# Weights in a new order on the ring: no loads beside the inverse and the chunk walk, values by token block, early output gate panels

## The chip, the cores and the metric

The kernel runs on one core of a Trainium2 chip. Its engines are TensorE (PE: matmuls, with its weight loads shown as PEld), VectorE (DVE), ScalarE (ACT), GpSimd (POOL) and SyncE (SP), which here issues the weight loads. The metric is device time in microseconds, the median of the runs.

## The reference

Two blocks work on x of 256 tokens by 1024 in float32. The first is RWKV-7 time mixing, a recurrence over the tokens, and then block-sparse attention; the second an mLSTM with an MLP and a latent attention (MLA) with an MLP, each modulated by rows that come from one vector c:

```python
x = x + rwkv7_time_mix(rms_norm(x, norm_a[i]), mu_a[i], w_in_a[i], ...)
...
x = x + moba_attention(rms_norm(x, norm_b[j]), w_in_b[j], q_norm_b[j], w_out_b[j], kb, vb, kmean, cos, sin)
...
cond = jax.nn.silu(c)
for l in range(DEPTH):
    ada = cond @ ada_w[l] + ada_b[l]
    sh1, sc1, g1, sh2, sc2, g2 = jnp.split(ada, 6, axis=-1)
    h = modulate(rmsnorm(x, norm_g[l, 0]), sh1, sc1)
    ...
    x = x + g1[:, None, :] * rmsnorm(y, norm_g[l, 1])
    h = modulate(rmsnorm(x, norm_g[l, 2]), sh2, sc2)
    y = sqrelu_mlp(h, mlp_w1[l], mlp_w2[l])
    x = x + g2[:, None, :] * rmsnorm(y, norm_g[l, 3])
```

## The kernel before

**Weights.** All weights come from memory in panels of 2 MB, in one fixed order (`order`), into a ring of four slots. SP issues panel i once panel i-4 is released (L1286 to L1292). A weight panel is worked on in two units. ScalarE writes the high part of a unit to a page (`split`, L1356, page_parts), VectorE writes the low part back into the ring slot (L2019, slot_parts), and TensorE does three matmuls for each product (`three`, L455 to L457: high by high, high by low, low by high). So a weight slot is released only by the last matmul that reads it. The 256 tokens are two token blocks of 128 (`tb`). Some products take each unit for both token blocks at once (`split_tok`, `split_T`), others go through a whole matrix for token block 0 and then again for block 1 (`split_blocks`), and a slot is then held until block 1 has used it; a function called between the units puts transposes there.

**Conditioning.** cond @ ada_w takes 28 panels of 512 columns. Most are summed on VectorE, a quarter of a panel at a time (`ada`, L1993, "ada_rows" in the order). Some go to TensorE (`ada_direct`, L595), 16 matmul records for a panel, and ScalarE copies the row (L1449), which TensorE turns to columns (`ada_turned`, L608). The row has one place in memory.

**The stages.** First block: projections; small 64x64 matmuls (L758) that build an inverse for each chunk; then the chunk walk, where the state goes from chunk to chunk (L813 to L900); wo_a; the attention; wo_b. SP holds conditioning panel 5 until the inverse's last step ("X", 5, 3), so the panels behind it load beside the chunk walk. Second block: norm and transposes of x (hT_c), q2, k2, gates, v2, then eight heads of mLSTM with the output gate's units (og) between them; then two direct conditioning panels, the transposes of the heads' output (h2T), and `mlp`: wo_c by token block, the new x and its norm, the transposes of block 0 (L537) ahead of wo_c's last unit for block 1, and the products up and w2 by turns. MLA and its MLP follow in the same way.

**What is fixed.** Each engine runs its instructions in the order they are written, and waits stand in them. ScalarE's and VectorE's splits are written out by hand among their other work: in `mlp` the splits of up's first panel stand ahead of the sum of squares of the branch's output (L1396). The gate rows of the second block go through eight diagonal matrices (`gate_diagonal`, L2469), which `spread` multiplies by ones.

## Time and profile before

| | before |
|---|---|
| median of 3 runs | 1048.17 us (1045.05 to 1049.97) |
| profiled execution: time, span | 1047.87 us, 1046.1 us |
| granted TensorE clock, mean | 0.99 |
| instructions | 19356 |
| DMA | 205.40 MB, 95 panels of 2048 KB |

The span is the time from the first to the last instruction in the trace, and t = 0 is its start. Times in the rows are microseconds. The busy share is an average over all stages: what stops TensorE has to be read stage by stage. A wait is put down to the engine that came last; "issue" stands for time in which the engine waited for nothing that the profile shows.

### The profile page before, as it was taken

Reading aid. Unit: us, or ns where it says so; the run is one execution under the profiler, and the core shown is the slowest. Engines: PE = TensorE matmul, PEld = TensorE weight load, DVE = VectorE, ACT = ScalarE, POOL = GpSimd, SP = SyncE. Lnnn points to the kernel's source line nnn. Section 1 sums busy time; section 2 is a strip of 40 time slices with the busy share of each in tenths; the row PEclk is TensorE's granted clock in tenths of the full one; section 3 lists DMA queues with packets and bytes.
Section 4 is the critical chain, followed back from the end, with each engine's and each line's share of the span. In section 5 each row is a group of like instructions: output and inputs, shape, how many; then the busy total and the mean of one; then the engine's idle time right before and its main releaser. Section 6 shows DMA issues by size and latency. Waiting matters only on the chain.

```text
span 1046.1 us, 19356 instructions
## 1 busy us (share of the span) xinstructions
PE 993.2 (95%) x8274; PEld 864.8 (83%) x8274; DVE 752.1 (72%) x1277; ACT 525.6 (50%) x798; POOL 36.4 (3%) x33
## 2 busy tenths in 40 slices
PE   5999999968999999999999999999999899999996
PEld 4788899967788888788867899999688788999995
DVE  6789889577889958646589665676587895664544
ACT  3358431316454677455366445454466855445442
POOL 0000044200000100000000000000000000000000
PEclk9999999999999999999999999999999999999999
DMA  9674410492456550564264477776646444476411
GB/s 379 248 284 161 162 43 4 162 389 100 154 211 219 221 242 11 232 242 161 81 242 161 170 294 303 287 291 264 240 164 215 188 161 161 172 296 256 171 72 41
DMA packets 15222, 205.40 MB, mean 196 GB/s; under 512 B 1816, under 2 KB 1816, under 8 KB 2976
## 3 DMA queue, kind: packets, MB, share of 16 engines
q1 hardware_dynamic: 14544, 202.55, 50.5%
q10 hardware_dynamic: 592, 1.61, 0.5%
q8 instruction: 66, 1.08, 0.4%
q14 instruction: 20, 0.16, 0.0%
HBM read 203.10 MB, written 1.05 MB: 195 GB/s over the span
## 4 chain that ended last, share of the span: by engine, by line
PE 83%; DVE 10%; ACT 3%; issue 2%; DMA 1%; SPq 0%; DVEq 0%; ACTq 0%
PE bank L455 20%; PE bank L457 20%; PE bank L456 20%; PE bank L758 5%; PE bank L404 4%; DVE slot_parts L2019 2%; PE bank L661 1%; PE bank L562 1%; DMA ring<-in_stream 1%; PE bank L739 1%; PE bank L634 1%; DMA pc<-in_params 1%; PE bank L623 1%; PE bank L900 1%; PE bank L537 1%
## 5 line engine op out<-in xcount | busy, mean ns | idle before, releaser
L455 PE MATMUL bank<-page_parts 128*128 128x512 f32 (+3 forms) x1222 | 428.8, 351 | 6.8 <-DVE page_parts L2301 2.2
L2019 DVE TENSOR_TENSOR slot_parts<-ring,page_parts 128x2048 fp32r<-128x2048 f32 (+2 forms) x117 | 261.4, 2251 | 53.4 <-ACT page_parts L1356 52.9
L457 PE MATMUL bank<-page_parts 128*128 128x512 f32 (+2 forms) x750 | 291.4, 389 | 0.0
L456 PE MATMUL bank<-slot_parts,page_parts 128*128 128x512 f32 (+2 forms) x750 | 290.9, 388 | 0.0
L455 PEld LDWEIGHTS bank<-page_parts 128*128 128x128 f32 x1222 | 232.3, 190 | 36.5 <-issue 3.7
L1356 ACT ACTIVATE page_parts<-ring 128x2048 fp32r<-128x2048 f32 (+2 forms) x121 | 225.0, 1884 | 52.6 <-PE bank L457 28.1
L457 PEld LDWEIGHTS bank<-page_parts 128*128 128x128 f32 x750 | 141.3, 188 | 29.0
L456 PEld LDWEIGHTS bank<-slot_parts,page_parts 128*128 128x128 f32 x750 | 141.8, 189 | 26.8
L1434 ACT ACTIVATE arena<-bank 128x512 f32<-128x512 f32 (+2 forms) x134 | 74.2, 575 | 127.2 <-PE bank L457 67.0
L457 PE MATMUL bank<-page_parts,slot_parts 128*128 128x256 f32 x472 | 133.6, 283 | 0.0
L456 PE MATMUL bank<-page_parts 128*128 128x256 f32 x472 | 133.6, 283 | 0.0
L1993 DVE CUSTOM_DVE_ANT_0 ring<-ring,small 128x1024 f32<-128x1024 f32 x88 | 104.1, 1229 | 0.0
L456 PEld LDWEIGHTS bank<-page_parts 128*128 128x128 f32 x472 | 90.6, 192 | 0.5
L457 PEld LDWEIGHTS bank<-page_parts,slot_parts 128*128 128x128 f32 x472 | 90.6, 192 | 0.0
L2573 DVE TENSOR_TENSOR page_parts<-arena,page_parts 128x512 fp32r<-128x512 f32 x24 | 16.6, 692 | 80.4 <-ACT page_parts L1773 80.4
L1769 ACT ACTIVATE arena<-bank 128x512 f32<-128x512 f32 x24 | 14.3, 597 | 117.4 <-PE bank L457 117.4
L758 PE MATMUL bank<-arena 64*64 64x64 f32 x1792 | 53.2, 219 | 2.0 <-issue 2.0
L758 PEld LDWEIGHTS bank<-arena 64*64 64x64 f32 x1792 | 52.8, 136 | 2.1 <-issue 2.1
L404 PE MATMUL bank<-arena,ring 128*128 128x256 f32 x192 | 41.9, 380 | 0.0
L404 PEld LDWEIGHTS bank<-arena,ring 128*128 128x128 f32 x192 | 36.4, 190 | 5.4 <-DMA ring<-in_stream 0.4
L562 PE MATMUL bank<-cc,arena 128*128 128x128 f32 x142 | 19.3, 292 | 18.2 <-DVE arena L1961 13.4
L2249 DVE TENSOR_TENSOR arena<-arena,bank 128x512 f32<-128x512 f32 x36 | 24.0, 683 | 16.9 <-PE bank L758 16.7
(318 smaller groups left out, 1114.2 us busy)
## 6 DMA issues: line engine op xcount, KB each, us to landing
ring<-in_stream SPq DMA_DIRECT2D x95, 2048.0 KB, 8.0
arena<-in_x SPq DMA_DIRECT2D x2, 512.0 KB, 4.3
arena<-in_gn ACTq DMA_DIRECT2D x2, 512.0 KB, 4.4
...
```

What stands on the lines that cost most here:

```text
L404: ins = mm(b[:, half * T:(half + 1) * T], weights[:, k, ct * P:(ct + 1) * P], src[:, k, :], start=(k == 0), stop=(k == k_tiles - 1))
L455: mm(out, a[0], b[0], start=start, stop=False)
L456: mm(out, a[0], b[1], start=False, stop=False)
L457: return mm(out, a[1], b[0], start=False, stop=stop)
L562: ins = nc.tensor.transpose(b[:, jj * T + tb * P:jj * T + (tb + 1) * P], src[:, tb, j * P:(j + 1) * P], ident)
L758: ins = mm(b[q * LC:(q + 1) * LC, j * LC:(j + 1) * LC], lhs(q, j), rhs(q, j), start=True, stop=True)
L1356: act(unit_parts(n)[0], unit_values(n)[1], ACT.Copy).then_inc(ac.step("w_hi"), 1)
L1434: act(dst, bank(product)[:, 0:n].rearrange("p (a b) -> p a b", a=dst.shape[1]) if len(dst.shape) == 3 else bank(product)[:, 0:n], kw.get(" ...
L1993: V.tensor_tensor_reduce(W, W, cond_row, 1.0, 0.0, ALU.mult, ALU.add, accum_out=ADA[:, at:at + 1]).then_inc(dv.step("ada_done" if ct == 3 ...
L2019: tt(unit_parts(n)[1], lo, hi, ALU.subtract).then_inc(dv.step("w_lo"), 1)
L2249: tt(dst[:, g], dst[:, g], bank((name, l, g))[:, :].rearrange("p (j t) -> p j t", j=8), ALU.subtract).then_inc(dv.frees((name, l, g)), 1)
L2573: tt(AF_LO[:, n % 2, 2 * i:2 * i + 2, :], a, hi, ALU.subtract).then_inc(dv.step("relu2"), 1)
```

## The change

1. **Ring and conditioning, first block.** Two panels, not six, are summed between g and wo_a. VectorE's 16 quarters in the inverse and the walk are gone. SP holds wo_a's second panel until chunk 2's state ("S", 2). The direct panel before yT is gone. In wo_a VectorE makes the low parts of yT ahead of a weight split, and ScalarE the high parts.
2. **Attention.** Three summed panels, not two, stand behind q1; VectorE sums 12 quarters there, not 8. ScalarE splits wo_b's first unit two heads later.
3. **wo_b and the mLSTM's entry.** wo_b goes by token block. hT_c is turned block by block, beside wo_b and v2. v2 comes first, by token block, then gates, q2, k2; og's panels are asked for before the heads.
4. **Gates.** One multiplication gives a column of eight gates; TensorE spreads it by a broadcast operand against the identity, with as many matmuls.
5. **Heads.** VectorE sums conditioning quarters in seven of the eight heads.
6. **MLP 0.** The ring's order at its entry is wo_c's first panel, direct, direct, wo_c's second; before it was direct, direct, and wo_c's two. Two more panels are summed in its loop.
7. **MLA.** Three direct panels, not two, two of them with four groups of 32 columns; three places for the row. One split is moved behind the norm of cq.

In all there are five direct and 23 summed panels, where there were six and 22. The diff, cut to its core:

```diff
@@ -500,12 +501,19 @@
                             ins.then_inc(filled((*name, 0)), 1)
                     ins.then_inc(unit_used((*name, 1) if i else None), 1)
-            def split_blocks(name, src, pages, ready, between=None, banks_of=None):
+            def block_panels(name, pages, after_first=None):
                 first, panels_of = len(units), []
                 for half in range(2):
                     split_panel((name, half), pages, by_k=True)
                     panels_of.append(order[-1])
+                    if half == 0 and after_first:
+                        after_first()
+                return first, panels_of
+            def split_blocks(name, src, pages, ready, between=None, banks_of=None, loaded=None):
+                first, panels_of = loaded or block_panels(name, pages)
                 for tb in range(TB):
                     bs = [claim((name, half, tb), None if banks_of is None else banks_of[2 * tb + half]) for half in range(2)]
...
-                i = ada_panel("ada")
-                ada_direct_of.append(i)
+                return slot, ada_panel("ada"), order[-1]
+            def ada_direct(reserved=None, pause=None, groups=2):
+                slot, i, entry = reserved or direct_panel()
+                ada_direct_of.append((i, groups))
                 b = claim(("ada_row", i))
                 pe.wait_ge(sem(f"slot_loaded{slot % SLOTS}"), 16 * (slot // SLOTS + 1))
                 W = ring[:, slot % SLOTS, :].rearrange("p (k n) -> p k n", k=KT)
+                width = P // groups
                 for k in range(KT):
...
+                    ins = mm(b[at:at + width, :], cond[:, k:k + 1].to_broadcast([P, width]), W[:, k, :], start=(k < groups),
+                             stop=(k >= KT - groups), tile_position=(0, at))
                 ins.then_inc(filled(("ada_row", i)), 1)
-                panel_used()
+                entry[1] = pn.last
             ada_turns = [0]
             def ada_turned():
...
@@ -748,7 +764,7 @@
             grams(1)
             turn("at", lambda j: AR[:, j, 0, :])
             project_rows("g", G_PAGES, 1)
-            ada(6)
...
-            ada_direct()
             turn_block("yT", Yr, 0, lambda g: (sem("y_gated"), g + 1))
             stage[0] = "attention"
             def beside_wo_a(tb, n):
-                if (tb, n) == (0, 1):
-                    ada_turned()
-                elif (tb, n) == (1, 0):
+                if (tb, n) == (1, 0):
                     turn_block("yT", Yr, 1, lambda g: (sem("y_gated"), 2 + g + 1))
                 elif (tb, n) == (1, 2):
...
                     ada(1)
-            ada(2)
...
@@ -974,24 +987,35 @@
             attention("at1", NH, HD, scores1, V1)
             transposes("o1T", O1, ready=lambda i: (sem("o1"), 1 + i // 3))
             stage[0] = "wo_b"
-            for half in range(2):
-                split_tok(("wo_b", half), split_parts(O1_PAGES), first_of(15, 16, 3), wait=("o1T_split", 0) if half == 0 else None)
+            def beside_wo_b(tb, n):
+                if (tb, n) == (1, 2):
+                    turn_block("hT_c", XN, 0, lambda g: (sem("xn"), 5))
+            def beside_v2(tb, n):
+                if (tb, n) == (0, 2):
+                    turn_block("hT_c", XN, 1, lambda g: (sem("xn"), 6))
+            def from_first(*pages):
...
                     for jj in range(4):
-                        pe.wait_ge(sem("diag"), 8 * i + 4 * half + jj + 1)
-                        ins = mm(b[:, jj * P:(jj + 1) * P], ones, DIAG[:, 4 * half + jj, :], start=True, stop=True)
+                        j = 4 * half + jj
+                        ins = mm(b[:, jj * P:(jj + 1) * P], gcol[:, j:j + 1].to_broadcast([P, P]), ident, start=True, stop=True)
                     ins.then_inc(filled(("gb", i, half)), 1)
...
             stage[0] = "mlstm"
-            for name in ("q2", "k2"):
-                split_T((name,), split_parts(MLSTM_PAGES), first_of(6, 14, 11), wait=("hT_c_split", 0) if name == "q2" else None)
-                if name == "q2":
-                    ada(1)
+            split_blocks("v2", split_parts(MLSTM_PAGES), from_first(6, 14, 1, 2), lambda tb, k: (sem("hT_c_split"), 2 * tb + k // 4 + 1),
+                         beside_v2)
             b = claim("gates")
...
+                ins.then_inc(filled("gate_cols"), 1)
+            ada(1)
+            split_T(("q2",), split_parts(MLSTM_PAGES), from_first(11, 16))
+            split_T(("k2",), split_parts(MLSTM_PAGES), from_first(13, 15), between=gate_columns)
+            og_pages = from_first(8, 11, 16, 13)
...
+                split_panel(("og", half), og_pages, by_k=True)
+            ada(2)
+            pe.wait_ge(*evacuated(("k2", 1)))
...
@@ -1173,17 +1192,20 @@
                     mm(b[:, 129:258], w[:, P:T], V2[:, 0, g, :], start=True, stop=False)
                     mm(b[:, 129:258], w[:, T:T + P], V2[:, 1, g, :], start=False, stop=True).then_inc(filled(("num", g)), 1)
             rotation["banks"] = kept
-            ada_direct()
-            ada_direct()
+            stage[0], reserved = "mlp0", []
+            loaded = block_panels("wo_c", from_first(15, 16, 3, 12), lambda: reserved.extend([direct_panel(), direct_panel()]))
+            for panel_of in reserved:
+                ada_direct(panel_of)
...
-            mlp(0, "wo_c", split_parts(H2_PAGES), "h2T_split", lambda tb, n: ada_turned() if (tb, n) == (0, 2) else None)
+            mlp(0, "wo_c", split_parts(H2_PAGES), "h2T_split", lambda tb, n: ada_turned() if (tb, n) == (0, 2) else None, loaded)
             ada_direct()
+            ada_direct(groups=4)
             stage[0] = "mla"
             q_a = split_spans("q_a", (0, 1536, 4, 15), (1536, 3072, 4, 16))
-            ada_direct((sem("x_sq"), 9))
...
@@ -1287,8 +1310,8 @@
                 if i >= SLOTS:
                     sp.wait_ge(*order[i - SLOTS][1])
-                if name == ("ada_rows", 5):
-                    sp.wait_ge(*finished(("X", 5, 3)))
+                if name == ("wo_a", 1):
+                    sp.wait_ge(*finished(("S", 2)))
                 sp.dma_start(ring[:, i % SLOTS, :], stream[i]).then_inc(sem(f"slot_loaded{i % SLOTS}"), 16)
...
             y_squares_of(1, 0)
             y_squares_of(1, 1)
-            split(unit_of["wo_a", 0] + 2)
-            ada_direct()
             halves_of("yT", 0, Y_PAGES)
             group_root(1)
             split(unit_of["wo_a", 0] + 3)
-            ada_turned()
             page_used.update({14: finished(("y", 1, 1)), 1: finished(("y", 1, 1)), 2: evacuated(("y", 1, 1)), 6: (sem("y_reduced"), 4)})
...
             page_used.update({p: finished(("v1", 1, 1)) for p in (15, 16)})
             u = unit_of["wo_b", 0]
-            attention("at1", NH, HD, 0.125, {n + 1: [(u + n // 4, n % 4)] for n in range(8)})
+            attention("at1", NH, HD, 0.125, {n + 3: [(u + n // 4, n % 4)] for n in range(8)})
...
                 if c == 2:
                     split(unit_of["wo_a", 0])
                 p = ("S", c)
@@ -2314,11 +2337,11 @@
             reduced(0)
             gated(0)
             group_norm(0)
-            split(unit_of["wo_a", 0] + 1)
             reduced(1)
             lows_of("yT", 0, Y_PAGES)
+            split(unit_of["wo_a", 0] + 1)
+            gated(1)
             split(unit_of["wo_a", 0] + 2)
-            gated(1)
             group_norm(1)
             lows_of("yT", 1, Y_PAGES)
...
             next_unit(("k1", 0, 0))
-            ada(8)
+            ada(12)
             def attention(name, heads, dvd, scale, O, early, between=None, gathered=None):
...
                     split(unit_of["cq"] + 1)
-            norm()
-            ada(2)
-            split_h("hT_c", MLSTM_PAGES)
-            for n in range(4):
-                next_unit(("q2", 0))
-                if n == 0:
-                    ada(2)
-                elif n == 1:
-                    modulation(4, 6, ())
-                    gate_diagonal(0)
+            modulation(4, 6, ())
+            gate_column(0)
+            u = unit_of["v2", 0]
+            for tb in range(TB):
+                add_to_x("wo_b", (tb,))
+                split(u + 2 * tb)
+                norm_block(tb)
+                split(u + 2 * tb + 1)
+                split_rows("hT_c", MLSTM_PAGES, 0, tb)
+            split(unit_of["q2",] + 1)
+            ada(4)
             dve.wait_ge(sem("gate_ln"), 1)
...
                         finish_head(g - 1)
+                if h < 7:
+                    ada(1 if h else 2)
                 if h == 7:
                     split(unit_of["wo_c", 0])
```

**VectorE, inverse's end to the chunk walk.** L2260 is the walk's preparation of a gate row, L1993 conditioning quarters (each with a short second instruction, left out here), L2312 the state's new value for a chunk. Before:

```order
L2260 TENSOR_TENSOR arena<-arena 128x1024 [waits dve_steps]
L1993 ISA ring,ADA<-ring,small 128x1024 [waits slot_loaded2]
L1993 ISA ring,ADA<-ring,small 128x1024
L1993 ISA ring,ADA<-ring,small 128x1024 [waits slot_loaded3]
L2312 TENSOR_TENSOR arena<-bank,small 128x512 [waits bank_full6]
L2260 TENSOR_TENSOR arena<-arena 128x1024
L1993 ISA ring,ADA<-ring,small 128x1024 [waits slot_loaded0]
L2312 TENSOR_TENSOR arena<-bank,small 128x512 [waits bank_full7]
L2019 TENSOR_TENSOR slot_parts<-ring,page_parts 128x2048 [waits w_hi]
L2312 TENSOR_TENSOR arena<-bank,small 128x512 [waits bank_full6]
```

Now, where L2284, L2335, L2045 and L2300 are the same lines as L2260, L2312, L2019 and L2276:

```order
L2284 TENSOR_TENSOR arena<-arena 128x1024 [waits dve_steps]
L2335 TENSOR_TENSOR arena<-bank,small 128x512 [waits bank_full6]
L2284 TENSOR_TENSOR arena<-arena 128x1024
L2335 TENSOR_TENSOR arena<-bank,small 128x512 [waits bank_full7]
L2045 TENSOR_TENSOR slot_parts<-ring,page_parts 128x2048 [waits w_hi]
L2335 TENSOR_TENSOR arena<-bank,small 128x512 [waits bank_full6]
L2300 TENSOR_REDUCE small<-arena 128x8 [waits y_square] x2
```

The quarters and their waits for slots are gone; the weight split stays between the second and third chunk.

**TensorE, from wo_b to the first product of the mLSTM.** L457 is the last of wo_b, L595 the direct panel, L562 the transposes of both blocks, L608 its row turned, L465 to L467 q2. Before, without repeats:

```order
L457 MATMUL bank<-page_parts 128x512
L595 MATMUL bank<-ring,small 64x512 [waits slot_loaded1,bank_free0]
L562 MATMUL bank<-cc,arena 128x128 [waits bank_free1,xn]
L562 MATMUL bank<-cc,arena 128x128 [waits bank_free2]
L562 MATMUL bank<-cc,arena 128x128 [waits bank_free3]
L608 MATMUL bank<-cc 128x1 [waits bank_free0,bank_free5]
L465 MATMUL bank<-page_parts 128x256 [waits hT_c_split,w_lo,bank_free6]
L466 MATMUL bank<-page_parts 128x256
L467 MATMUL bank<-page_parts,slot_parts 128x256
```

Now, the transposes (L545) of block 0 stand in wo_b's second block, v2's first unit (L454 to L456) follows wo_b at once, and block 1's transposes stand after v2's second unit:

```order
L545 MATMUL bank<-cc,arena 128x128 [waits xn,bank_free6]
L545 MATMUL bank<-cc,arena 128x128 [waits xn,bank_free7]
L454 MATMUL bank<-page_parts 128x512
L454 MATMUL bank<-page_parts 128x512
L454 MATMUL bank<-page_parts 128x512 [waits w_lo,hT_c_split,bank_free1,bank_free0]
L454 MATMUL bank<-page_parts 128x512 [waits hT_c_split,w_lo]
L545 MATMUL bank<-cc,arena 128x128 [waits xn,bank_free2]
L545 MATMUL bank<-cc,arena 128x128 [waits xn,bank_free3]
L454 MATMUL bank<-page_parts 128x512 [waits w_lo]
```

The direct panel and its row are gone, and so is the place where TensorE has nothing but transposes to do.

**ScalarE, the entry of MLP 0.** L1356 splits wo_c, and from the x2 row on up's first panel; L1449 copies a conditioning row, L1462 scales h2T, L1396 is the sum of squares of wo_c's output. Before, without repeats:

```order
L1356 ACTIVATE page_parts<-ring 128x2048 [waits pe_steps,slot_loaded3]
L1356 ACTIVATE page_parts<-ring 128x2048 [waits bank_full1,slot_loaded0]
L1449 ACTIVATE cc<-bank 128x512 [waits bank_full2]
L1462 ACTIVATE arena<-bank,pc 128x256 [waits bank_full4]
L1442 ACTIVATE ADA<-bank 128x4 [waits bank_full0]
L1449 ACTIVATE cc<-bank 128x512 [waits bank_full3]
L1356 ACTIVATE page_parts<-ring 128x2048 [waits bank_full1,slot_loaded0]
L1442 ACTIVATE ADA<-bank 128x4 [waits bank_full4]
L1356 ACTIVATE page_parts<-ring 128x2048 [waits bank_full1,slot_loaded1] x2
L1396 ACTIVATE arena,small<-bank 128x512 [waits bank_full0]
L1396 ACTIVATE arena,small<-bank 128x512 [waits bank_full1]
```

Now (L1379, L1474, L1487, L1465 and L1419 are the same lines):

```order
L1379 ACTIVATE page_parts<-ring 128x2048 [waits pe_steps,slot_loaded2]
L1379 ACTIVATE page_parts<-ring 128x2048 [waits bank_full3,slot_loaded1]
L1474 ACTIVATE cc<-bank 128x512 [waits bank_full6]
L1487 ACTIVATE arena<-bank,pc 128x256 [waits bank_full0]
L1465 ACTIVATE ADA<-bank 128x4 [waits bank_full4]
L1474 ACTIVATE arena<-bank 128x512 [waits bank_full7]
L1379 ACTIVATE page_parts<-ring 128x2048 [waits bank_full3,slot_loaded1]
L1465 ACTIVATE ADA<-bank 128x4 [waits bank_full4]
L1379 ACTIVATE page_parts<-ring 128x2048 [waits bank_full3,slot_loaded2] x2
L1419 ACTIVATE arena,small<-bank 128x512 [waits bank_full0]
L1419 ACTIVATE arena,small<-bank 128x512 [waits bank_full1]
```

The rows and their order are the same; the slots that the splits wait for are others. The panels in the ring, each with the panel whose slot it takes:

```
before: direct <- v2_0, direct <- v2_1, wo_c0 <- og0, wo_c1 <- og1, up00 <- direct, up01 <- direct, w2_0 <- wo_c0, summed <- wo_c1, up02 <- up00
after:  wo_c0 <- og0, direct <- og1, direct <- summed, wo_c1 <- summed, up00 <- wo_c0, up01 <- direct, summed <- direct, w2_0 <- wo_c1, summed <- up00, up02 <- up01
```

## Rows read from the trace of the kernel before

**Rows 1.** The page: busy time of each engine.
```profile
PE 993.2 (95%) x8274; PEld 864.8 (83%) x8274; DVE 752.1 (72%) x1277; ACT 525.6 (50%) x798; POOL 36.4 (3%) x33
```
**Rows 2.** Windows: stretch, us, busy PE, PEld, DVE, ACT, POOL, PEclk, DMA share, GB/s.
```profile
145.30:197.50 52.20, 52.20 (x1792) 52.20 (x1793) 43.40 (x59) 14.87 (x26) 22.31 (x16) 1.00 0.07 21
203.60:249.30 45.70, 33.49 (x986) 32.42 (x982) 29.19 (x46) 11.64 (x18) 0.00 (x0) 0.89 0.71 286
```
**Rows 3.** TensorE's waits, 197 to 250: total, times, longest; largest and smallest of six.
```profile
PE bank L838 <- issue: 2.9, 1, 2.9
...
PE bank L838 <- DVE arena L2312: 0.8, 1, 0.8
PE bank L827 <- issue: 0.7, 1, 0.7
```
**Rows 4.** Windows in the chunk walk: first and last of three slow stretches, then full clock.
```profile
206.80:210.20 3.40, 3.40 (x71) 3.40 (x69) 2.79 (x4) 0.00 (x0) 0.00 (x0) 0.50 1.03 439
...
237.50:240.90 3.40, 3.27 (x62) 3.27 (x64) 2.01 (x1) 1.35 (x1) 0.00 (x0) 0.51 0.05 14
240.90:249.30 8.40, 8.24 (x292) 8.06 (x289) 5.59 (x13) 4.93 (x7) 0.00 (x0) 1.00 0.01 4
```
**Rows 5.** Panel loads of L1292, 197.5 to 199.9: durations, first and last start, landing.
```profile
L1292 SPq DMA_DIRECT2D ring<-in_stream x4: 328/434/516, 197.8 to 199.2; - x4
...
DMA to landing us min/median/max: 8.6/15.3/22.0
```
**Rows 6.** TensorE's timeline before wo_a: start, us, line, shapes, idle before.
```profile
249.27 3.65 PE L595 MATMUL bank<-ring,small 128*64 128x512 f32 x16
252.85 1.09 PE L537 MATMUL bank<-cc,arena 128*128 128x128 f32 x8
255.09 0.47 PE L455 MATMUL bank<-page_parts 128*128 128x512 f32 x1 [1.15 <-DVE page_parts L2301]
```
**Rows 7.** TensorE's timeline from wo_b to q2.
```profile
426.89 0.39 PE L456 MATMUL bank<-slot_parts,page_parts 128*128 128x512 f32 x1
427.12 0.39 PE L457 MATMUL bank<-page_parts 128*128 128x512 f32 x1
427.43 3.65 PE L595 MATMUL bank<-ring,small 128*64 128x512 f32 x16
...
435.54 0.36 PE L465 MATMUL bank<-page_parts 128*128 128x256 f32 x1 [0.69 <-DVE page_parts L2066]
```
**Rows 8.** VectorE's timeline before the first head.
```profile
479.56 8.90 DVE L2019 TENSOR_TENSOR slot_parts<-ring,page_parts 128x2048 fp32r<-128x2048 f32 x4 [3.62 <-ACT page_parts L1356]
```
**Rows 9.** VectorE's timeline in the MLA: the gate diagonals.
```profile
763.54 1.66 DVE L2469 TENSOR_SCALAR arena<-cc,small 128x128 f32<-128x128 f32 x8
```
**Rows 10.** TensorE's longest wait in the MLA, 740 to 800.
```profile
PE bank L562 <- DVE arena L2696: 1.7, 1, 1.7
```
**Rows 11.** Panel loads of L1292, 520 to 524.5, columns as in rows 5.
```profile
L1292 SPq DMA_DIRECT2D ring<-in_stream x1: 327/327/327, 523.4 to 523.4; - x1
...
DMA to landing us min/median/max: 7.8/7.8/7.8
```
**Rows 12.** SP's timeline, 550 to 560.
```profile
556.56 0.33 SPq L1292 DMA_DIRECT2D ring<-in_stream  x1
```
**Rows 13.** ScalarE's timeline at wo_c.
```profile
531.20 1.91 ACT L1356 ACTIVATE page_parts<-ring 128x2048 fp32r<-128x2048 f32 x1 [1.11 <-DMA ring<-in_stream]
...
534.21 3.02 ACT L1462 ACTIVATE arena<-bank,pc 128x256 f32<-128x256 f32 x8 [0.61 <-PE bank L562]
...
547.13 3.71 ACT L1356 ACTIVATE page_parts<-ring 128x2048 fp32r<-128x2048 f32 x2
```
**Rows 14.** The chain of waits, 520 to 562: start, us, what.
```profile
537.35 0.49 PE bank L455
...
560.42 1.06 PE bank L537 x8
```
**Rows 15.** Windows: the slow stretch in wo_c, columns as in rows 2.
```profile
537.90:541.30 3.40, 3.40 (x9) 2.63 (x8) 3.37 (x4) 1.68 (x1) 0.00 (x0) 0.50 0.86 369
```

193 lines of the change are left out of this document (95 added, 98 removed).

## The prediction

> **What bounds the kernel now.** I read the page's busy shares first: TensorE is busy 95% of the span [rows 1]. So the time is TensorE's work plus the places where it stands still, and a change pays only where it takes one of those away, or costs where it makes one. Then I looked for the places by the busy time of stretches and by TensorE's waits in them. Two are large. One is the chunk walk of the first block (203.6 to 249.3), where TensorE is busy 33.49 of 45.70 us while the inverse before it, with 1792 matmuls in 52.20 us, has no gap at all [rows 2]. The other is the border between wo_b and the mLSTM, 427.5 to 435.5 [rows 7]. Third I read the ring, since the change puts its panels in another order: each panel is issued only when the panel four places ahead of it has been released, and SP issues strictly in that order, so a late release also holds all that stand behind it.
>
> **A. No load in the walk: -13.3.** In the walk the waits name "issue", six of them from 2.9 to 0.7 us, together 11.3 us [rows 3]; the inverse has none. They are not waits for data. What differs is the load: the four panels issued at 197.8 to 199.2 [rows 5] keep the DMA engines 71% busy there, against 7% in the inverse [rows 2]. Beside them TensorE fell three times to a granted clock of 0.50 (1.2 GHz) for 3.4 us; there 71 or 62 matmuls were done where 8.40 us at full clock hold 292, or 28.8 ns each [rows 4]. That is 2.0 and 1.8 us of work in 3.4, so a stretch costs some 1.4 and the three 4.0. Without both: 45.7 - 11.3 - 4.0 = 30.4 us; from the other side 986 matmuls by 28.8 ns and 1.0 us of waits on VectorE and banks make 29.4, so the two agree. Gain 15.3. The new hold lets wo_a's second panel and k1's go once chunk 2's state is done, some 6.6 us before the walk's end. One issue wait of the mean size (11.3/6 = 1.9) comes back: 13.3. Bounds: 0 if the waits do not come from the loads, 15.3 if none comes back.
>
> The Trainium skill ("Runtime: NRT & Kernel Launch", Instruction fetch mechanics) says that instructions are fetched block by block by the engine's own queue, and that this is hidden because the engine dispatches more slowly than the fetch fills. By that rule no issue wait could come from a load, and A would be the clock's 4.0 at most. The trace speaks against it here: six such waits of 11.3 us with loads, none without [rows 2, 3].
>
> VectorE loses 16 quarters of conditioning (the ISA rows at L1993) in inverse and walk. TensorE waits for VectorE only 0.8 us in the walk, so I count nothing.
>
> **B. Direct panel off, VectorE's order in wo_a: -1.4.** Before wo_a TensorE ran 16 matmuls for a conditioning row (3.65 us), turned yT (1.09) and then waited 1.15 for VectorE's low part [rows 6]. Without the 3.65 us TensorE stands ready earlier, but the chain y, norm, low part on VectorE hardly moves; what moves is that the low part of yT now stands ahead of a weight split of 2.3 us (L2019). I take 1.4 of the 3.65+1.15; bounds 0 and 4.8.
>
> **C. wo_b by token block, values first: -3.1.** Between wo_b's last matmul (427.12, the next 0.23 later, as 426.89 to 427.12 shows) and q2's first stand 8.0 us: the direct panel's 3.65, then turns and small matmuls with waits for VectorE, the last of 0.69 [rows 7]. In the new order the two turns stand inside wo_b and v2, 2 x 1.09 [rows 6], so 8.0 - 2.2 = 5.8 goes. Against it: VectorE's four og splits end at 488.5, where the first head's work starts, and the last split was preceded by a wait of 3.62 for ScalarE [rows 8]; so 3.6 is all that VectorE can be brought forward, and with TensorE there 5.8 earlier it comes 2.2 late. ScalarE's halves of wo_b begin two heads later in the attention: 0.5 for the first unit. Together -5.8+2.2+0.5 = -3.1. Bounds -5.8 and +2 (the norm of block 0 has two units of 12 matmuls by 0.23 as cover, 5.5 us; if it needs 8, 2.5 comes back at each of the two turns).
>
> The gate's eight multiplications (1.66 us together) become one; TensorE's matmuls stay as many. In the MLA the eight [rows 9] stand ahead of a wait of TensorE of 1.7 [rows 10], which G counts; at the other places TensorE's waits name nothing near them, so they count nothing.
>
> **D. wo_c's second panel comes third: +9.7.** Before, the ring had direct, direct, wo_c0, wo_c1; now wo_c0, direct, direct, wo_c1. The slot that came free last was og1's, at 523.41. Then only wo_c1 waited for it, and landed 7.8 us later at 531.2 [rows 11]. Now the first direct panel stands in that slot, and behind it on SP the second and wo_c1: all three leave at 523.4 to 524. Queued panels land one by one: of the four at 197.8 to 199.2 the first took 8.6, the last 22.0 [rows 5], so 206.4 and 221.2 and 4.9 us between two. So 531.6, 536.5 and 541.4. ScalarE splits wo_c1's first half before it copies the conditioning row and scales h2 [rows 13] (the order of both kernels stands under the change): 541.4 + 1.91 + 0.6 = 543.9 for the scaling against 534.21, and TensorE's first wo_c matmul stood 3.14 behind that, at 537.35 [rows 14]: 547.0, 9.7 later. The two direct panels, on TensorE from 531.6 and 536.5, are through by then (3.65 each).
>
> **E. The MLP's first panel waits for wo_c0: +17.2 more.** up(0,0) had a direct panel's slot, free before wo_c begins. Now it has wo_c0's, which is released when TensorE has gone through that panel for the second token block; before, this release let another panel go at 556.56 [rows 12]. With D: 556.56 + 9.7 = 566.2, landed 7.8 later, 574.0. On ScalarE the two splits of that panel stand ahead of the squares of the branch's output, and VectorE's low parts stand ahead of its sums, and both are ahead of the new x, its norm and the turn. Before, from the start of that split (547.13, [rows 13]) to the turn (560.42, [rows 14]) it took 13.3 us, all of it work in a row. 574.0 + 13.3 = 587.3, against 560.42: 26.9 in all, 17.2 beyond D. TensorE stands at that turn, with only the last unit of wo_c ahead.
>
> **F. What follows: +3.4.** up(0,2) has up(0,1)'s slot and not up(0,0)'s. Between the two only w2's first panel is left, 48 matmuls by 0.23, 10.9 us, and the load (7.8), issue (0.3), high and low splits (1.9+2.3) make 12.3: +1.4, with what is queued on SP 1.7. And after 18 us of standing TensorE a slow stretch is likely: before, one came at 537.90 after the short gaps there, 3.4 us at 0.50 [rows 15], so 1.7.
>
> **G. MLA: +0.3.** A third direct panel takes the slot of w2's last, whose release comes late in the MLP, and its load of 7.8 [rows 11] is likely to end about 1 us behind the place where TensorE wants it; the gate's shorter work and the split moved behind cq's norm take part of the 1.7 wait [rows 10]. Bounds -1 and +2. The direct panels in four groups of 32 columns have no row: at least 8 matmuls of 0.23 (1.83), as the present form's 16 records in 3.65 show half that rate; I take 1.83 and keep 7.3 (twice the old) as the other end, which is in the range.
>
> The Trainium skill ("TensorEngine Tiling (Array Packing)", When to Use Tiling) names four column groups for a stationary side of 32 columns. By it four of the matmuls run side by side, a quarter of the time. The row with two groups shows 3.65 us for 8 products of 512 columns [rows 7], which is no better than one after another; by the rule the sum would be lower by up to 2.
>
> Sum: -13.3 -1.4 -3.1 +9.7 +17.2 +3.4 +0.3 = +12.8 us. The profiled span of 1046.1 becomes 1058.9; that execution took 1047.87, 1.8 more than its span and 0.3 under the median of 1048.17. So 1060.7, and I say 1061.
>
> **Rivals.**
> 1. *The MLP's first panel is not late* (the other side). If its slot comes free by 549, so that it has landed when ScalarE gets to it (547.13 + 9.7 = 556.9), E's 17.2 falls: 1061 - 17 = 1044, and 2.2 of F with it (no long stand, no slow stretch): 1042, faster by 0.6%. For it: only the release rule holds it, no data. Against it: the low part of wo_c0 is written into its slot and read until the second block's matmuls are through, and the old release of that panel is seen at 556.56 [rows 12]. It decides from 549; each us behind that costs one. Chance 0.09, a third of it over 1042.9.
> 2. *The issue waits do not come from the loads.* Then A gives nothing: 1061 + 13 = 1074. For it: no row says what was fetched. Against it: rows 2 and 3. Chance 0.04.
> 3. *The loads at the walk's tail give back more.* Three panels now land beside some 6.6 us of small matmuls; two waits of the largest size (2.9) and a slow stretch (1.4) are 7.2 against the 1.9 counted: 1066. Chance 0.10.
> 4. *Part of E is absorbed.* Of the 13.3 us behind the split some 4 to 8 may run beforehand, if ScalarE's and VectorE's first work is short once their buffers are free, and some of F's 3.4 with it: 1050 to 1055. For it: TensorE finished block 0 of wo_c long before. Against it: the order on both engines is fixed. Chance 0.10, of which 0.02 below 1050.
>
> **How the numbers follow.** My forecast has 0.67, and by itself 1055 to 1067: A from -9 to -15.3, C and G by their bounds. The range of 1051 to 1069 takes in rivals 3 and 4 but for the lowest edge, and leaves out 1 and 2. A measurement of this kernel tells 0.5%, 5.2 us, from no change: same is 1043 to 1053.4. Slower: 0.65 of the forecast, 0.10 and 0.04 of rivals 3 and 2, 0.03 of rival 4: 0.82. Same: 0.05 of rival 4, 0.02 of the forecast, 0.03 of rival 1: 0.10. Faster: 0.06 of rival 1 and 0.02 of rival 4: 0.08.
>
> **What would show it.** A: no issue waits between inverse and 240, and a walk of 31 to 33 us. B and C: TensorE's gaps before wo_a and q2 gone, the first head's work on VectorE starts 16 to 19 us earlier than 488.4. D: three panels issued within 1 us of og1's release, 4.9 us apart in landing, and wo_c's first matmul 23 to 24 us behind that release, where it was 13.9 (523.41 to 537.35). E: SP issues up(0,0) when block 1 has gone through wo_c0, ScalarE waits for the DMA, and TensorE stands 16 to 20 us at the turn of block 0. If that gap is under 5 us, the prediction is wrong, and the time is near 1042. If the issue waits are still there, it is near 1074.

## The result and the profile after

| | before | after |
|---|---|---|
| median | 1046.93 us (1045.05 to 1049.97, 4 runs) | 1075.61 us (1071.57 to 1078.74, 4 runs) |
| ratio, 95% interval | | 1.0263 (1.0239 to 1.0286) |
| profiled execution: time, span | 1047.87, 1046.1 us | 1074.64, 1072.8 us |
| TensorE busy | 993.2 us | 993.2 us |
| granted TensorE clock, mean | 0.99 | 0.97 |

The kernel became slower by 2.6%, 28.7 us in the medians. The direction was forecast, the size was not: 1061 with a range to 1069. TensorE is busy for the same time, 993.2 us, so what the kernel lost is time in which TensorE stands. The page of the kernel after; its busy times and the clock in 40 slices:

```profile
PE 993.2 (93%) x8250; PEld 863.7 (81%) x8250; DVE 751.4 (70%) x1266; ACT 524.2 (49%) x797; POOL 34.8 (3%) x33
...
PEclk9999999999999999999787999999879999999999
```

The clock dips at two places, slices 20 to 22 (mlstm's end and MLP 0's entry) and 29 to 30 (the MLA's entry). Those are the places where TensorE stands. Its waits over the whole kernel after, greatest first (total, times, longest):

```profile
PE bank L545 <- DVE arena L1998: 19.0, 2, 18.7
PE bank L570 <- DVE arena L1987: 15.5, 2, 11.5
PE bank L608 <- DMA ring<-in_stream: 9.9, 2, 5.8
PE bank L639 <- ACT arena L1682: 6.5, 9, 1.5
```

The first is the stand that term E forecast. Of the second, 11.5 us stand at the start (11.7 in the kernel before), 4.07 at the MLA's entry. The third is the two sets of direct panels. The fourth is the first attention.

Where the shift between the two traces grows, read from the start of the same work in each:

| start of | before | after | shift | change here | forecast |
|---|---|---|---|---|---|
| wo_a | 255.09 | 238.22 | -16.9 | -16.9 | A, B: -14.7 |
| transposes behind the first attention | 402.35 | 391.90 | -10.5 | +6.4 | +0.5, in C |
| first head's output | 486.86 | 469.94 | -16.9 | -6.4 | C without that 0.5: -3.6 |
| last head's output | 524.82 | 509.94 | -14.9 | +2.0 | 0 |
| wo_c | 537.35 | 531.53 | -5.8 | +9.1 | D: +9.7 |
| turn of block 0 | 560.42 | 573.11 | +12.7 | +18.5 | E: +17.2 |
| end of MLP 0 | 746.95 | 763.60 | +16.7 | +4.0 | F: +3.4 |
| transposes in the MLA | 755.67 | 780.87 | +25.2 | +8.5 | G: +0.3, with the row below |
| attention in the MLA | 807.36 | 834.76 | +27.4 | +2.2 | |
| end | 1046.1 | 1072.8 | +26.7 | -0.7 | |

**Chunk walk.** The window of the walk and TensorE's waits in it (against [rows 2, 3]):

```profile
206.40:234.60 28.20, 26.79 (x927) 26.13 (x923) 14.18 (x20) 11.37 (x17) 0.00 (x0) 1.00 0.23 80
```
```profile
PE bank L854 <- DVE arena L2335: 1.1, 2, 0.8
...
PE bank L854 <- issue: 0.2, 1, 0.2
```

Full clock, and no issue wait to speak of. The two windows do not hold the same work: that of before begins with an issue wait of 1.97 and the last 52 matmuls of the inverse. From the walk's first matmul to its last it is 41.7 us before (207.52 to 249.27) and 28.4 after (206.15 to 234.57). With the time of those 52 matmuls (1.5 us) the stretch of 45.7 us now takes 29.9, where 30.4 was worked out without any issue wait and 32.3 with one. At the walk's end the kernel is 14.7 us ahead (A: -13.3); it would be 15.8, but the inverse began 1.1 us later (146.33 against 145.24), a shift of which 0.8 is there by 30 us, ahead of anything that the change touches. From there to wo_a it gains 2.2 more (B: -1.4).

**MLP 0's entry.** SP's loads, TensorE and ScalarE (against [rows 11, 12, 14, 13]):

```profile
L1315 SPq DMA_DIRECT2D ring<-in_stream x3: 327/430/432, 508.5 to 509.4; - x3
...
DMA to landing us min/median/max: 8.0/13.4/17.7
```
```profile
531.53 0.47 PE L454 MATMUL bank<-page_parts 128*128 128x512 f32 x1 [0.90 <-DVE page_parts L2092]
...
573.11 1.94 PE L545 MATMUL bank<-cc,arena 128*128 128x128 f32 x8 [18.68 <-DVE arena L1998]
```
```profile
527.07 1.91 ACT L1379 ACTIVATE page_parts<-ring 128x2048 fp32r<-128x2048 f32 x1 [11.86 <-DMA ring<-in_stream]
...
559.82 3.71 ACT L1379 ACTIVATE page_parts<-ring 128x2048 fp32r<-128x2048 f32 x2 [17.43 <-DMA ring<-in_stream]
563.44 0.58 ACT L1419 ACTIVATE arena<-bank 128x512 f32<-128x512 f32 x1
```

Three panels leave together and land some 5.3 us apart (8.0 and 17.7 us after issues 0.9 apart). wo_c begins 23.0 us behind og1's release (forecast 23 to 24). The split of up(0,0) waits 17.43 us for its panel, and the squares of wo_c's output, ready long before, come behind it. From that split to the turn it takes 13.3 us (559.82 to 573.11), the same as before. From 573.1 to 577.3 the granted clock is 0.50, which makes 2.1 of F's 4.0.

**What the forecast did not have.** The same at the MLA's entry, ScalarE:

```profile
766.26 2.86 ACT L1379 ACTIVATE page_parts<-ring 128x1536 fp32r<-128x1536 f32 x2 [18.74 <-DMA ring<-in_stream]
769.03 0.58 ACT L1442 ACTIVATE arena<-bank 128x512 f32<-128x512 f32 x1
```

q_a was issued at 753.20 (before: 725.3), and its split waits for it until 766.26. MLP 0's output was complete at 763.7, its first block earlier, but its squares (L1442) stand behind that split, and the norm and the transposes behind them. TensorE meanwhile had the third direct panel, and that was late too; and the clock fell:

```profile
763.60 5.51 PE L608 MATMUL bank<-ring,small 128*64 128x512 f32 x32
773.15 3.64 PE L608 MATMUL bank<-ring,small 128*32 128x512 f32 x16 [4.05 <-DMA ring<-in_stream]
780.87 3.46 PE L570 MATMUL bank<-cc,arena 128*128 128x128 f32 x15 [4.07 <-DVE arena L1987]
```

From 771.9 to 788.9 the granted clock is 0.50, where the kernel before has 1.00 at this place; the 2.2 us behind the transposes stand in that stretch, and no run takes them apart. In the first attention VectorE waits, 357 to 393:

```profile
DVE slot_parts L2032 <- ACT page_parts L1392: 6.5, 2, 3.7
```

The kernel before has no such wait there. VectorE's quarters of wo_b stayed at heads 6 to 13 while ScalarE's moved from heads 1 to 8 to heads 3 to 10; a quarter's low part waits for the whole unit's high part, so VectorE waits at its heads 6 and 10 (3.7 and 2.8 us), and ScalarE waits 4.2 us for VectorE.

### The profile page after: what moved, and what is told of

Same layout as the page of the kernel before. It is cut to its first block, busy times and chain, and to the rows that moved or that the text cites. A ratio compares the mean times of both kernels' runs of the same rounds, so it can differ in the third digit from the quotient of the medians.

```text
span 1072.8 us, 19297 instructions
## 1 busy us (share of the span) xinstructions
PE 993.2 (93%) x8250; PEld 863.7 (81%) x8250; DVE 751.4 (70%) x1266; ACT 524.2 (49%) x797; POOL 34.8 (3%) x33
## 4 chain that ended last, share of the span: by engine, by line
PE 79%; DVE 9%; DMA 6%; ACT 4%; issue 2%; SPq 0%; ACTq 0%; DVEq 0%
PE bank L454 19%; PE bank L456 19%; PE bank L455 19%; PE bank L774 5%; DMA ring<-in_stream 5%; PE bank L403 4%; DVE slot_parts L2045 3%; PE bank L677 1%; ACT page_parts L1379 1%; PE bank L570 1%; PE bank L755 1%; PE bank L545 1%; ACT arena L1457 1%; DMA pc<-in_params 1%; PE bank L1015 1%
## 5 line engine op out<-in xcount | busy, mean ns | idle before, releaser
L454 PE MATMUL bank<-page_parts 128*128 128x512 f32 (+2 forms) x1238 | 435.0, 351 | 10.6 <-DVE slot_parts L2045 3.2
L2045 DVE TENSOR_TENSOR slot_parts<-ring,page_parts 128x2048 fp32r<-128x2048 f32 (+2 forms) x117 | 261.5, 2250 | 89.8 <-ACT page_parts L1379 89.2
L456 PE MATMUL bank<-page_parts 128*128 128x512 f32 (+2 forms) x750 | 292.3, 390 | 0.0
L1379 ACT ACTIVATE page_parts<-ring 128x2048 fp32r<-128x2048 f32 (+2 forms) x121 | 224.6, 1884 | 104.3 <-DMA ring<-in_stream 80.2
L454 PEld LDWEIGHTS bank<-page_parts 128*128 128x128 f32 x1238 | 236.0, 191 | 42.5 <-issue 8.4
L456 PEld LDWEIGHTS bank<-page_parts 128*128 128x128 f32 x750 | 142.2, 190 | 29.2
L455 PE MATMUL bank<-page_parts 128*128 128x256 f32 x488 | 138.1, 283 | 0.0
L456 PE MATMUL bank<-page_parts,slot_parts 128*128 128x256 f32 x488 | 138.1, 283 | 0.0
L2019 DVE CUSTOM_DVE_ANT_0 ring<-ring,small 128x1024 f32<-128x1024 f32 x92 | 109.0, 1229 | 5.8 <-DMA ring<-in_stream 5.8
L455 PEld LDWEIGHTS bank<-page_parts 128*128 128x128 f32 x488 | 93.6, 192 | 0.5
L456 PEld LDWEIGHTS bank<-page_parts,slot_parts 128*128 128x128 f32 x488 | 93.6, 192 | 0.0
L570 PE MATMUL bank<-cc,arena 128*128 128x128 f32 x126 | 19.1, 312 | 16.7 <-DVE arena L1987 15.5
```

The costliest lines, as they stand in the source:

```text
L454: mm(out, a[0], b[0], start=start, stop=False)
L455: mm(out, a[0], b[1], start=False, stop=False)
L456: return mm(out, a[1], b[0], start=False, stop=stop)
L570: ins = nc.tensor.transpose(b[:, jj * T + tb * P:jj * T + (tb + 1) * P], src[:, tb, j * P:(j + 1) * P], ident)
L1379: act(unit_parts(n)[0], unit_values(n)[1], ACT.Copy).then_inc(ac.step("w_hi"), 1)
L2019: V.tensor_tensor_reduce(W, W, cond_row, 1.0, 0.0, ALU.mult, ALU.add, accum_out=ADA[:, at:at + 1]).then_inc(dv.step("ada_done" if ct == 3 ...
```

## The experiments

The theory after the result: the walk's gain is as forecast and comes from the loads; the loss is one mechanism at several places, **a weight panel that lands late is split ahead of a norm or a head's work on ScalarE and VectorE, and holds these**. E saw it at one place. The rival: clock, DMA contention, or VectorE's added conditioning. Runs with one execution are set against the profiled execution of the kernel after, 1074.64 us. The four executions of that kernel lie 7.2 us apart (1071.57 to 1078.74), so where a total differs by less (e3, e4, e5, e8) it decides nothing by itself, and the stage in the trace has to.

**e1_entry.**
```diff
-            stage[0], reserved = "mlp0", []
-            loaded = block_panels("wo_c", ..., lambda: reserved.extend([direct_panel(), direct_panel()]))
+            stage[0], reserved = "mlp0", [direct_panel(), direct_panel()]
+            loaded = block_panels("wo_c", from_first(15, 16, 3, 12))
```


> The changed kernel with the ring order of before at MLP 0's entry: direct, direct, wo_c0, wo_c1. Theory (the stand of 18.7 us at the turn of block 0 is up(0,0)'s late slot, term E): up(0,0) has the first direct panel's slot again and lands by 532, the stand falls under 2 us; wo_c still begins near 531, since three panels still wait behind og1 (term D stays); up(0,2) has its old slot: 18.5 + 1.4 + 1.7 = 21 us less, near 1054. Rival (the norm chain, not the panel, makes the stand): the stand stays over 10 us, the time over 1070.

1064.27 us, 10.4 less and not 21. TensorE:
```profile
526.97 0.77 PE L1191 MATMUL bank<-arena 128*128 128x129 f32 x2 [16.84 <-DVE arena L2675]
...
566.99 1.07 PE L545 MATMUL bank<-cc,arena 128*128 128x128 f32 x8 [1.17 <-DVE arena L1998]
```
The stand at the turn is 1.17 where it was 18.68: E is right. But a stand of 16.84 appeared ahead of the last head. ScalarE and VectorE split wo_c's first unit inside the heads, and that panel now lands last; ScalarE waited 17.8 us for it. The same mechanism at a third place, which I had not seen when I wrote the expectation.

**e2_norm_first.** In MLP 0 on ScalarE (VectorE likewise):
```diff
-                split(first + 1)
                 y_block(branch, 0)
-                split(first + 2)
                 x_block_squares(0)
+                split(first + 2)
```


> The changed kernel; in MLP 0 alone ScalarE and VectorE work on block 0's branch output, new x and norm first, and split up(0,0)'s units behind that. The panel stays as late as it is. Theory (a late panel is so dear because its split stands ahead of the norm): the turn comes near 553 to 556 where it was 573.1, then TensorE waits for the split panel (landed 559.8, split 564) and up begins near 567 where it was 575: 7 to 10 us less, near 1067. Rival (only the landing counts, and TensorE would wait for the panel as long anyway): up begins at 574 to 576, no change, 1074 to 1077.

The MLP behind the MLA keeps its order. 1066.56 us, 8.1 less. TensorE, and the same place in the kernel after:
```profile
551.92 1.04 PE L545 MATMUL bank<-cc,arena 128*128 128x128 f32 x8
...
569.12 0.76 PE L454 MATMUL bank<-page_parts 128*128 128x512 f32 x1 [13.43 <-DVE page_parts L2554]
```
```profile
574.71 0.78 PE L454 MATMUL bank<-page_parts 128*128 128x512 f32 x1
...
578.76 0.40 PE L454 MATMUL bank<-page_parts 128*128 128x512 f32 x1
```
TensorE now takes the turn and the last unit of wo_c first and waits 13.43 for up's first product. What begins at 574.71 in the kernel after, behind its turn, is still wo_c's last unit; up's first product begins there at 578.76. So it begins 9.6 us earlier in e2 (the expectation took 575 for it), and the turn of block 1 still 7.7 earlier (579.28 against 586.94). The panel's lateness stays; its place in the order was worth some 8 of the 18.5.

**e4_quarters8.**
```diff
-            attention("at1", NH, HD, 0.125, O1, quarters_from(6, u, 1), gathered=gate_o1)
+            attention("at1", NH, HD, 0.125, O1, quarters_from(8, u, 1), gathered=gate_o1)
```


> The changed kernel with VectorE's early quarters of wo_b at heads 8 to 15 of the first attention, where they were at 6 to 13 (ScalarE's halves stay at 3 to 10). Theory (the attention takes 31.9 us where it took 26.0 because VectorE's first quarter of each unit now waits for ScalarE's last quarter of that unit, 3.7 and 2.8 us, and ScalarE then waits for VectorE): the two waits go, the attention takes 27 to 28 us, the time is 4 to 5 less, near 1071. Rival (the late landing of wo_b makes it): only the 1.1 us wait for the DMA matters, the attention still takes 31 us, no change.

1068.96 us, 5.7 less. VectorE has no wait for ScalarE's quarters left, and the transposes stand at 386.54 where they stood at 391.90. But e4 was already 1.25 us earlier when its attention began. From the attention's first matmul to the transposes it is 29.2 us before (from 373.14), 35.1 after (from 356.81) and 31.0 in e4 (from 355.56): 4.1 of the 5.9 are this, and 1.8 remain that no run explains.

**e6_qa_third and e5_qa_second.** e6: q_a ahead of all three direct panels, and the third one's matmuls behind the transposes:
```diff
+            stage[0] = "mla"
+            q_a = split_spans("q_a", (0, 1536, 4, 15), (1536, 3072, 4, 16))
             ada_direct()
             ada_direct(groups=4)
-            stage[0] = "mla"
-            q_a = split_spans("q_a", (0, 1536, 4, 15), (1536, 3072, 4, 16))
-            ada_direct(groups=4)
+            third = direct_panel()
             pe.wait_ge(sem("xn"), 10)
             transposes("hT_d", XN)
             ada_turned()
+            ada_direct(third, groups=4)
```
e5: the same, but q_a stands behind the first direct panel:
```diff
             ada_direct()
-            ada_direct(groups=4)
             stage[0] = "mla"
             q_a = split_spans("q_a", (0, 1536, 4, 15), (1536, 3072, 4, 16))
             ada_direct(groups=4)
+            third = direct_panel()
...
+            ada_direct(third, groups=4)
```


> The changed kernel with q_a asked for ahead of the direct panels of the MLA, and the third direct panel's matmuls behind the transposes of x. Theory (q_a lands at 766.2, its split stands on ScalarE ahead of the squares of MLP 0's output, and all of the norm is late by that, the same mechanism as in MLP 0's entry): q_a lands near 750, the squares begin within 2 us of MLP 0's last matmul, the transposes of x stand near 772 where they were at 780.9, 8 to 9 us less, near 1067. Rival (TensorE's clock and the loads beside it make the 10 us): the transposes stay over 778, no change.

1086.04 us, 11.4 more. TensorE:
```profile
774.48 3.67 PE L570 MATMUL bank<-cc,arena 128*128 128x128 f32 x16 [3.21 <-DVE arena L1988]
...
803.17 1.87 PE L624 MATMUL bank<-cc 128*128 128x1 f32 x8 [11.03 <-ACT arena L1888]
```
The transposes stand 8.7 us behind MLP 0's end where they stood 17.3, and the squares of the first block begin at 759.74, ahead of MLP 0's end. The run made two edits, though: it also took the third direct panel out of TensorE's way. In the kernel after that panel was through at 776.79 (about 775.0 at full clock), so with q_a early and the panel left where it was, the transposes could have come 4 to 6 us earlier, not 8.6, by my estimate from these times. The late q_a sets the time of 780.87; the late third panel stands close behind it, and the two were not run apart. kv_a now has q_a's own slot, lands late, and its split stands on ScalarE ahead of the second half of scaled x (L1888), and TensorE waits 11.0 for that. A fourth place, made by my own edit. (Some 2 us of the 11.4 stand ahead of MLP 0's end, 765.75 against 763.60.)

> The changed kernel with q_a behind the first direct panel of the MLA and the third one's matmuls behind the transposes, so that kv_a, unlike in e6, has a direct panel's slot and not q_a's. Theory (the one late panel ahead of the norm is worth 8 us net): the transposes of x begin 8 to 9 us earlier than 17.3 behind MLP 0's last matmul, no wait of 11 us for kv_a's split, the time is 1065 to 1068. Rival (the norm's gain turns into a wait for kv_a or for the third direct panel further on): over 1071.

With kv_a in a direct panel's slot again it took 1070.82 us, 3.8 less and not 8. The transposes stood at 774.88, 11.6 behind MLP 0's end and not 8.7, since q_a, second in the ring, landed only shortly ahead of that end; of these 5.7 us the third direct panel, now behind the transposes, takes back its own time (1.92); what else makes the difference to 3.8 was not traced.

**b_entry.** The kernel before, with the ring order wo_c0, direct, direct, wo_c1 at MLP 0's entry (the edit of e1 the other way).

> The kernel before with one thing of the change: the ring order wo_c0, direct, direct, wo_c1 at MLP 0's entry. Here only wo_c1 waits behind og1, so term D should be absent, and up(0,0) waits for wo_c0's release. Theory (E by itself): wo_c begins at 537 as before, up(0,0) is issued at 556.6 and lands at 564.4, the turn of block 0 stands at 577 to 578 where it stood at 560.4, and with w2's and up(0,2)'s later slots 17 to 21 us more: 1065 to 1069. Rival (the ring order costs only where three panels queue, as D): the turn moves by under 3 us, 1048 to 1052.

1065.68 us, 17.8 over the profiled execution of before. up(0,0) was issued at 553.9 and TensorE did this:
```profile
534.71 0.50 PE L455 MATMUL bank<-page_parts 128*128 128x512 f32 x1 [0.82 <-ACT ADA L1455]
...
575.58 1.73 PE L544 MATMUL bank<-cc,arena 128*128 128x128 f32 x7 [18.99 <-DVE arena L1985]
```
wo_c is not late (534.71 against 537.35), the turn is: 40.9 us behind wo_c's start where it was 23.1. The order of four panels in the ring alone costs 18 us, two thirds of the whole change.

**e3_load_in_walk and e8_load_in_inverse.**
```diff
                 if name == ("wo_a", 1):
-                    sp.wait_ge(*finished(("S", 2)))
+                    sp.wait_ge(*finished(("X", 5, 3)))
```


> The changed kernel with its hold on wo_a's second panel ended where the kernel before ended its own, at the inverse's last step, so three panels (wo_a1, k1_0, k1_1) load beside the chunk walk, and VectorE still has no conditioning there. Theory (the issue waits and the slow clock of the walk come with the loads): issue waits of 5 to 9 us and one or two stretches at half clock come back, the walk takes 35 to 41 us where it takes 28.2, the time is near 1083. Rival (they came with VectorE's conditioning quarters, which are absent here): no issue wait over 0.5 us, the walk takes 28 to 29, the time stays at 1074 to 1076.

1081.22 us, 6.6 more, and TensorE's issue waits are back, in the inverse's last step and in the walk, though VectorE has no conditioning there:
```profile
PE bank L843 <- issue: 3.0, 1, 3.0
PE bank L774 <- issue: 2.1, 1, 2.1
...
PE bank L865 <- issue: 0.8, 1, 0.8
```
From 206.6 to 240.7 it is 34.1 us, under the 35 to 41 expected, and the clock stays at 1.00. So the waits come with the loads. The three slow stretches of before, 4.0 of the 15.3 in A, do not come back with them, and the third of those had a DMA share of 0.05 beside it [rows 4]: what made them is open. e8 takes the hold away altogether.

> The changed kernel with no hold at all: the three panels wo_a1, k1_0 and k1_1 are asked for as soon as their slots are free, near 140, and land by some 160, inside the inverse, whose 64x64 matmuls run at the same rate as the walk's and which had no wait in either kernel. Theory (the issue waits are TensorE's own instruction blocks of 16 KB, which come late when panels stand in the DMA engines: such a block starts every 3.7 us in the walk without loads and every 6.1 to 6.7 us beside them): two or three issue waits of 1 to 3 us appear in the inverse between 140 and 160, with none in the walk; 3 to 6 us more than the 1074.6 of the changed kernel's profiled execution. Rival (the waits belong to what the walk does, its dependences on VectorE and ScalarE): the inverse stays without waits, and the time is 1073 to 1075.

1079.34 us, 4.7 more. The inverse, which had no wait between 145 and 197 in either kernel, has three, and behind the first of them a slow stretch:
```profile
PE bank L774 <- issue: 4.1, 3, 1.9
```
```profile
155.40:158.80 3.40, 3.40 (x71) 3.40 (x68) 1.16 (x2) 0.38 (x1) 0.96 (x1) 0.50 1.06 447
```
What is waited for is seen in the DMA queues: the rows of the instruction queue (q8; packets, MB, share), 206 to 237, before and after:
```profile
q8 instruction: 5, 0.08, 0.9%
```
```profile
q8 instruction: 7, 0.11, 1.6%
```
In the same 31 us seven blocks of 16 KB came without loads, and five beside them; for 140 to 165 it is four in the kernel after and three in e8. By itself this could be an effect of the standing and not its cause. The times settle it (q8 in narrow windows). In the kernel before a block starts to move at 203.3, 209.4, 215.6, 222.2, 228.9 and 235.3, and TensorE's six issue waits end at 205.64, 211.74, 217.93, 224.40, 231.24 and 237.63; in e8 it is 151.6, 158.2 and 163.3 against 153.87, 160.51 and 165.53. Every issue wait of 0.7 us or more in the walk and the inverse of these runs, the three of e3 too, ends 2.2 to 2.6 us behind the start of such a block.

**b_walk.** The kernel before with the first part alone, and the four displaced panels at the attention's entry (one) and in MLP 0 (three).
```diff
-            ada(6)
+            ada(2)
...
-            ada(2)
+            ada(3)
...
+        ada_before_down = ((1, 4, 8), ())
...
-                if name == ("ada_rows", 5):
-                    sp.wait_ge(*finished(("X", 5, 3)))
+                if name == ("wo_a", 1):
+                    sp.wait_ge(*finished(("S", 2)))
```


> The kernel before with the first part of the change alone: two summed panels behind g, no conditioning on VectorE in inverse and walk, the hold on wo_a's second panel until chunk 2's state; of the four panels displaced one goes to the attention's entry and three into MLP 0's loop. Everything from wo_b on is as before, the ring order at MLP 0's entry too. Theory (A alone is worth 15 to 17 us and the change lost it downstream): 1031 to 1034. Rival (the displaced panels cost in MLP 0 what the walk gives, VectorE being late there): the walk is as short, MLP 0 is 5 us longer or more, 1037 to 1045.

1048.99 us, ratio 1.0008 (0.9994 to 1.0022): the same as before. wo_a began 12.2 us earlier (242.94), but wo_b landed later in the attention, where TensorE waits 3.80, and the shift was 6.8 behind it. MLP 0 took 190.2 us from the turn to its end (553.65 to 743.86) where it had taken 186.5, and the MLA's entry took 3.4 more, where ScalarE waited 13.6 us for q_a:
```profile
370.88 0.87 PE L624 MATMUL bank<-cc,arena 128*128 128x128 f32 x3 [3.80 <-ACT arena L1663]
...
743.86 6.22 PE L596 MATMUL bank<-ring,small 128*64 128x512 f32 x26
753.38 2.63 PE L596 MATMUL bank<-ring,small 128*64 128x512 f32 x6 [3.29 <-ACT arena L1386]
```
That is neither the theory's 1031 to 1034 nor the rival's 1037 to 1045. Of the 12.2 us the attention takes back 5.4, MLP 0 3.7 and the MLA's entry 3.4: the four panels taken out of the walk, with the hold that came with them, cost as much behind it. The two were not run apart.

**a_best.** The four late places mended together:
```diff
-            ada(2)
+            reserved = [direct_panel(), direct_panel()]
...
-                if h < 7:
-                    ada(1 if h else 2)
...
-        ada_before_down = ((1, 8), ())
+        ada_before_down = ((1, 3, 5, 8), ())
```
with e4's and e5's edits, and VectorE's 40 quarters in MLP 0 by twos.

> The changed kernel with its four late places mended: the two direct panels stand right behind og's in the ring, so that wo_c0, wo_c1 and up(0,0) have the slots of og0, og1 and the first direct panel, as before; the two summed panels of the heads go into MLP 0's loop; wo_b's early quarters on VectorE stand at heads 8 to 15; q_a is asked for behind the first direct panel of the MLA, and the third one's matmuls stand behind the transposes. Theory (D 9, E 18.5, F 4, heads 2, attention 5.6, MLA 8.6, less up to 5 for VectorE's 8 more quarters in MLP 0): 1027 to 1033, faster than before by 1.5%. Rival (VectorE becomes the bound of MLP 0 with ten panels of conditioning): MLP 0 is 8 us longer or more and the time is over 1036.

1044.10 us, ratio 0.9962 (0.9944 to 0.9980): faster than before, by less than expected. The turn stood at 542.28, 18.1 earlier than before, but MLP 0 took 192.6 us, 6.1 more, and the MLA's entry 3.4 more. The rival had the time right and not the reason. In MLP 0 ScalarE waits 64.4 us for weight panels (14.2 before) and VectorE 44.2 for ScalarE: the panels are late, VectorE is not the bound.

**a_best4 and a_best5.** Four groups of 32 columns for all direct panels; a_best4 also spreads VectorE's quarters over all units.
```diff
-                ada_direct(panel_of)
+                ada_direct(panel_of, groups=4)
...
-        {u: 2 for u in range(4, 30) if u % 4 > 1 or u in (4, 5, 8, 9, 16, 17, 28, 29)}
+        {u: 2 if u % 4 > 1 or u > 27 else 1 for u in range(4, 30)}
```


> a_best with its five direct panels all in four groups of 32 columns, and VectorE's 40 conditioning quarters in MLP 0 spread over all units (one with most, two with fourteen) where they stood by twos. Theory (MLP 0 is 6 us longer than before because quarters by twos make the low parts late, ten waits of 1 us): 3 to 4 us less there, and up to 2 for the direct panels where VectorE doesn't bound: 1038 to 1041. Rival (VectorE has too much in MLP 0 whatever the spread, or a quarter now waits for its panel): 1043 to 1048.

1070.23 us, 1.0214 (1.0187 to 1.0242). The turn came at 537.87, 4.4 earlier than in a_best. All was lost behind it, in MLP 0:
```profile
PE bank L454 <- DVE slot_parts L2044: 25.4, 9, 6.1
```
VectorE itself waited 81.6 us there for ScalarE's splits (44.2 in a_best), and ScalarE 109.5 for panels (64.4). The time is over both ranges, the rival's too. That a summed panel held its slot longer and the weights behind it came late is my reading; a_best5, which differs from this run in the spread alone, shows what the spread costs but not by which slot.

> a_best with its direct panels in four groups of 32 columns, and VectorE's conditioning quarters in MLP 0 by twos as in a_best (not spread as in a_best4). Theory (the four groups took the turn of block 0 from 542.3 to 537.9 in a_best4, and what a_best4 lost stood in MLP 0 alone, where spread quarters held the ring's slots and the weight panels behind them came late): the turn at 538, MLP 0 again near 192 to 193 us, 1038 to 1041, faster than before by 0.7 to 1%. Rival (the four groups' gain is given back where VectorE is late in MLP 0, since it has the same work in less time): 1043 to 1045, as a_best.

1042.27 us, ratio 0.9935 (0.9915 to 0.9956), the lowest of all, a little over the theory's range. So the spread alone made 28 us of a_best4's time. The turn stood at 541.84 and not at 538: the direct panels began at 508.05, 3.0 later than in a_best, and from their start to the turn it took 33.8 us (37.2 in a_best, 33.2 in a_best4). MLP 0 took 192.3. At that place the four groups are worth 3 to 4 us; in the time the intervals of a_best and a_best5 overlap, so their gain there is not settled. Two direct panels took 3.64 us there (508.05 to 511.69), where two in two groups took 7.09 in the kernel before (525.65), but the transposes behind them then waited 2.63 for VectorE.

## Why the prediction was wrong

**A and B were right**, in size (16.9 against 14.7) and in the larger part of the mechanism. The issue waits come with loads (e3), in the inverse too (e8), so rival 2 is out; the loads at the walk's tail brought back none over 0.2 us, where I took one of 1.9, so rival 3 is out. The 4.0 us for the slow stretches went as well, but I put them to the loads and e3 does not bear that out. The page's rule fails here: the Trainium skill ("Runtime: NRT & Kernel Launch", Instruction fetch mechanics) has the fetch hidden by the dispatch rate, and beside panel loads it is not (11.3 us of waits before, 5.9 in e3, 4.1 in e8).

**C was mis-sized in two parts, with different signs.** The border gave 6.4 where I took 3.6: VectorE was not 2.2 late. (The gap that I read as 8.0 is 8.2 by its rows.) Up to the attention's end 6.4 were lost where I took 0.5 "for the first unit", 5.9 of them inside the attention. I looked at ScalarE's halves and not at the partner on VectorE whose quarters had not been moved; e4 gives back 4.1 of the 5.9.

**D, E and F were right**: 9.1, 18.5, 4.0 against 9.7, 17.2, 3.4. e1, e2 and b_entry show the cause; rivals 1 and 4 are out as far as block 0's norm cannot begin before the split. Of F, 2.1 were the slow stretch behind the turn (forecast 1.7); the rest was not taken apart.

**The heads** cost 2.0 where I named nothing. That VectorE's eight quarters stand in a chain that TensorE waits for is likely and was not run by itself.

**G is the step that failed**, 0.3 forecast, 10.0 measured at the end. I weighed the third direct panel, the one that is in the diff, and took its load to end about 1 us late; TensorE waited 4.05 for it. The panel that set the time was q_a, which the change does not touch but pushes one place back in the ring: issued at 753.2, landed at 766.2, and split ahead of the squares of MLP 0's output. This is E's mechanism at the next stage's entry; I had used it once and not asked at which other norm a split stands first. 8.5 of the 10.0 stand ahead of the transposes, and 8.6 go when q_a is early and the third panel's matmuls stand behind them (e6); by the same estimate q_a alone is worth 4 to 6 of them. With the attention's 5.9 this is why the time left the range.

The forecast of four groups at 1.83 us a panel was right: one panel of each form in a row takes 5.51. The reading of "no better than one after another" for two groups was wrong, since the 0.23 us of a record, my measure, belong to another data type (fp32r). The float32 matmuls of 256 columns take 0.218 us a record (L404 in the kernel before, 64 records in 13.98), so a record of 512 would take some 0.44 one after another; in two groups it takes 0.228 and in four 0.114, a half and a quarter. The Trainium skill ("TensorEngine Tiling (Array Packing)", When to Use Tiling) names these factors, 2x for a stationary side of 64 columns and 4x for one of 32, and the trace agrees.
